# Order of single waits in a two-block transformer kernel: gates, last pair and first pair of the softmax attentions, their projection, banks of the second queries, last token tiles

## The reference

```python
def first_block(x, ...):
    z = rms_norm(x, norm1_g) @ w_in                      # glu | q | k | v | gate logits
    a = silu(rms_norm(causal_depthwise_conv(a_val * sigmoid(a_gate)), conv_norm_g))   # 31 taps
    y_a = a @ w_conv_out
    # three dilated window attentions over 16 heads of 64, mixed by the softmax of their log-sums
    o = einsum('gbsh,gbshd->bshd', softmax(stack(lses)), stack(outs))
    y_b = o @ w_attn_out
    g_a, g_b = split(sigmoid(gate_logits + gate_b))
    x = x + (g_a * y_a + g_b * y_b) @ w_out
    u_val, u_gate = split(causal_depthwise_conv(rms_norm(x) @ w_up))                  # 3 taps
    return x + (silu(u_gate) * u_val) @ w_down

def second_block(x, ...):
    # layer 0: softmax attention over the 128 keys that an index score picks; times silu(g); projection
    # layer 1: stick-breaking attention; times silu(g); projection
    # each followed by layer_norm(ALPHA * x + y)
```

## Time and profile before

| what | value |
|---|---|
| median of 3 runs | 1572.48 us (1572.32 to 1574.3) |
| profiled execution, its time | 1572.18 us |
| its span (first to last instruction) | 1570.4 us |
| PE busy | 1520.5 us, 97% of the span |
| DVE busy | 907.5 us, 58% |
| ACT busy | 520.4 us, 33% |
| POOL busy | 547.1 us, 35% |
| chain that ended last | PE 90%, DVE 5%, DMA 2%, ACT 2%, issue 1% |
| mean granted clock of PE | 0.994 of full speed |

### The profile page before, as it was taken

One profiled execution on the slowest core, in us unless ns is written; L12 is line 12 of the kernel. 1 busy time (PEld: TensorE's weight loads), 2 busy tenths in 40 slices (PEclk: granted clock), 3 DMA queues, 4 the chain that ended last, 5 costly groups with the idle time before them and its releaser, 6 DMA issues.

```text
span 1570.4 us, 19211 instructions
## 1 busy us (share of the span) xinstructions
PE 1520.5 (97%) x7506; PEld 1240.4 (79%) x7506; DVE 907.5 (58%) x1562; ACT 520.4 (33%) x1012; POOL 547.1 (35%) x662
## 2 busy tenths in 40 slices
PE   6999999999999999999999999999999989999996
PEld 5888888877777788888888887787777868888885
DVE  2899968478864243334310025896887451767765
ACT  4223234267741132222200012212776032444440
POOL 3222234421124444444444443344111334332221
PEclk9999999999999999999999999999999999999999
DMA  8999998854349788898988887788333768665655
GB/s 230 191 199 192 192 192 191 187 121 94 80 100 208 170 179 190 192 195 197 192 190 194 184 184 161 158 189 185 68 81 71 181 143 191 131 136 116 133 119 136
DMA packets 72969, 253.10 MB, mean 161 GB/s; under 512 B 7728, under 2 KB 11952, under 8 KB 72880
## 3 DMA queue, kind: packets, MB, share of 16 engines
q0 software_dynamic: 66528, 242.25, 71.4%
q1 hardware_dynamic: 5808, 7.53, 1.4%
q10 hardware_dynamic: 544, 2.10, 0.4%
HBM read 249.75 MB, written 2.10 MB: 160 GB/s over the span
## 4 chain that ended last, share of the span: by engine, by line
PE 90%; DVE 5%; DMA 2%; ACT 2%; issue 1%; POOL 0%; SPq 0%; DVEq 0%; ACTq 0%; POOLq 0%
PE PSUM L485 26%; PE PSUM L487 25%; PE PSUM L486 25%; PE PSUM L684 3%; PE PSUM L642 2%; PE PSUM L660 2%; PE PSUM L791 1%; PE PSUM L809 1%; PE PSUM L822 1%; PE PSUM L630 1%; DMA W_LO<-wstream 1%; DMA SMALLS<-small 1%; PE PSUM L956 1%; DVE QKV L1538 0%; PE PSUM L673 0%
## 5 line engine op out<-in xcount | busy, mean ns | idle before, releaser
L473 POOL DMA_DIRECT2D W_HI<-wstream x231 | 131.0, 567 | 860.9 <-PE PSUM L487 860.4
L485 PE MATMUL PSUM<-X_HI,W_HI 128*128 128x512 f32 x872 | 347.8, 399 | 4.0 <-DVE X_LO L1428 2.7
L487 PE MATMUL PSUM<-X_HI,W_LO 128*128 128x512 f32 x872 | 340.0, 390 | 0.0
L486 PE MATMUL PSUM<-X_LO,W_HI 128*128 128x512 f32 x872 | 339.9, 390 | 0.0
L465 POOL DMA_DIRECT2D W_LO<-wstream x231 | 206.9, 896 | 106.5 <-POOL W_LO L462 84.1
L462 POOL TENSOR_SCALAR W_LO<-W_HI 128x1024 fp32r<-128x1024 f32 x195 | 212.4, 1089 | 28.7 <-DMA W_HI<-wstream 25.5
L485 PE MATMUL PSUM<-W_HI,X_HI 128*128 128x512 f32 x544 | 212.8, 391 | 1.1 <-ACT QKV L1296 1.1
L486 PE MATMUL PSUM<-W_LO,X_HI 128*128 128x512 f32 x544 | 211.7, 389 | 0.0
L487 PE MATMUL PSUM<-W_HI,X_LO 128*128 128x512 f32 x544 | 211.7, 389 | 0.0
L485 PEld LDWEIGHTS PSUM<-X_HI,W_HI 128*128 128x128 f32 x872 | 163.3, 187 | 45.5 <-issue 9.2
L487 PEld LDWEIGHTS PSUM<-X_HI,W_LO 128*128 128x128 f32 x872 | 163.3, 187 | 35.2
(11 more groups left out here) (227 smaller groups left out, 2355.7 us busy)
## 6 DMA issues: line engine op xcount, KB each, us to landing
W_HI<-wstream POOLq DMA_DIRECT2D x231, 512.0 KB, 3.8
W_LO<-wstream POOLq DMA_DIRECT2D x231, 512.0 KB, 5.6
GATE_A<-x SPq DMA_DIRECT2D x4, 512.0 KB, 5.9
QKV<-x SPq DMA_DIRECT2D x8, 256.0 KB, 3.2
NORM_GAINS<-lnv ACTq DMA_DIRECT2D x2, 1024.0 KB, 6.5
out<-GATE_B SPq DMA_DIRECT2D x3, 512.0 KB, 2.6
CONST<-consts SPq DMA_DIRECT2D x1, 968.0 KB, 10.6
out<-GATE_B SPq DMA_DIRECT2D x2, 256.0 KB, 2.0
```

The costliest lines, as they stand in the source:

```text
L473: pool.dma_start(W_HI[:, n % SLOTS, :], wstream[n]).then_inc(w_hi_in[n % SLOTS], 16)
L485: pe.matmul(o, lh, rh, start=start, stop=False)
L486: pe.matmul(o, lh, rl, start=False, stop=False)
L487: return pe.matmul(o, ll, rh, start=False, stop=stop)
```

## The change

Six edits, all of order; no arithmetic, no instruction and no DMA is added or removed.

1. Gates of "a": DVE's `gates(i, 3)` moves from the end of pair i into pair i+1, behind its first `biased`, the reciprocal (`inverse`) and the two `pt_lo` of query block 2.
2. Last pair of "b": on ACT `pt_hi(7, 0)` and `pt_hi(7, 1)` come ahead of `low_products(6)`; on DVE `pt_lo(7, 0)`, `pt_lo(7, 1)` and `biased(7, 3)` come ahead of `both_parts(6)`.
3. First pair of both: PE's `turn_qk(1, 1)` moves behind `turn_p(0, 0)` and `turn_p(0, 1)`.
4. `attention_out`: each slab runs k = 0 to 7 in one go, slabs 0 and 1 too.
5. Second half of q2: one wait for each bank instead of one for all four.
6. out_b, second half: slab 2 runs for token tiles 0 and 1 before slab 3 is waited for.

(Edit 1 also stands behind the loop for pair 7, whose gate slab has no work for DVE.)

```diff
@@ t_half @@
-                pe.wait_ge(tile_free, free)
+                if not by_bank:
+                    pe.wait_ge(tile_free, free)
...
+                            if by_bank and k == 0:
+                                pe.wait_ge(tile_free, free - TT + 1 + t)
...
                 if tokens:
+                    if paired:
+                        slab_ready(s0 + kts // 2 - 2)
+                        products(kts // 2 - 2, 0)
+                        products(kts // 2 - 2, 1)
                     for t in range(TT):
                         for n in (kts // 2 - 2, kts // 2 - 1):
+                            if paired and t < 2 and n == kts // 2 - 2:
+                                continue
@@ softmax_attention, PE @@
-                    if i < PAIRS - 1:
+                    if 0 < i < PAIRS - 1:
                         turn_qk(i + 1, 1)
                     turn_p(i, 0)
                     turn_p(i, 1)
+                    if i == 0:
+
+                        turn_qk(1, 1)
@@ attention_out @@
-                for n in range(2):
-                    slab_ready(s0 + n)
-                    part(n, range(KT - 1))
-                for n in range(2):
-                    part(n, (KT - 1,)).then_inc(slab_done, 1)
-                pe.wait_ge(tile_free, t0)
-                for n in range(2, KT):
+                for n in range(KT):
+                    if n == 2:
+                        pe.wait_ge(tile_free, t0)
                     slab_ready(s0 + n)
                     part(n, range(KT)).then_inc(slab_done, 1)
@@ attention, ACT @@
-                    if i:
+                    if a == "b" and i == PAIRS - 1:
+                        pt_hi(i, 0)
+                        pt_hi(i, 1)
                         low_products(i - 1)
-                    pt_hi(i, 0)
-                    pt_hi(i, 1)
+                    else:
...
@@ attention, DVE @@
                         pt_lo(i - 1, 2, 0)
                         pt_lo(i - 1, 2, 1)
+                        if a == "a":
+                            gates(i - 1, 3)
...
-                    if i:
+                    if a == "b" and i == PAIRS - 1:
+
+                        pt_lo(i, 0)
+                        pt_lo(i, 1)
+                        biased(i, 3)
                         both_parts(i - 1)
-                    biased(i, 3)
-                    pt_lo(i, 0)
-                    pt_lo(i, 1)
+                    else:
...
-                    gates(i, 3)
+                    if a == "b":
+                        gates(i, 3)
```

More of the change, by code:

```diff
@@ L542, in f_phase, with t_half @@
                     turn(i, False)
-            def t_half(bank, s0, kts, hi, lo, free, ready=None, tokens=None, aside=None, slabs=None):
-                pe.wait_ge(tile_free, free)
+            def t_half(bank, s0, kts, hi, lo, free, ready=None, tokens=None, aside=None, slabs=None, by_bank=False, paired=False):
+                if not by_bank:
+                    pe.wait_ge(tile_free, free)
                 banks = bank if isinstance(bank, tuple) else range(bank, bank + TT)
@@ L868, in stick_attention @@
                 pe.wait_ge(sem("c_wt_lo"), 4 * PAIRS)
-                t_half(OUT_B_BANKS[1], s0 + KT // 2, KT, O_HI, O_LO, t0, tokens="out_b_token")
+                t_half(OUT_B_BANKS[1], s0 + KT // 2, KT, O_HI, O_LO, t0, tokens="out_b_token", paired=True)
             pe.wait_ge(const_in, 32)
@@ L965, in _ @@
             index_scores(0)
-            t_half(4, s0 + 4, KT, X_HI, X_LO, t0 + 4, scores_beside)
+            t_half(4, s0 + 4, KT, X_HI, X_LO, t0 + 4, scores_beside, by_bank=True)
             need(pe, "i_relu", 3 * IH)
@@ L1139, in attention @@
                         qk_hi(i + 1, 1)
-                    if i:
+                    if a == "b" and i == PAIRS - 1:
+                        pt_hi(i, 0)
+                        pt_hi(i, 1)
                         low_products(i - 1)
-                    pt_hi(i, 0)
-                    pt_hi(i, 1)
+                    else:
+                        if i:
+                            low_products(i - 1)
+                        pt_hi(i, 0)
+                        pt_hi(i, 1)
                     prob(i, 3, 0)
@@ L1572, in attention @@
                         qk_lo(i + 1, 1)
-                    if i:
+                    if a == "b" and i == PAIRS - 1:
+                        pt_lo(i, 0)
+                        pt_lo(i, 1)
+                        biased(i, 3)
                         both_parts(i - 1)
-                    biased(i, 3)
-                    pt_lo(i, 0)
-                    pt_lo(i, 1)
+                    else:
+                        if i:
+                            both_parts(i - 1)
+                        biased(i, 3)
+                        pt_lo(i, 0)
+                        pt_lo(i, 1)
                     if i:
```

## The result

| | kernel before | changed kernel |
|---|---|---|
| median, 5 runs each | 1573.69 us (1572.32 to 1574.3) | 1565.18 us (1562.48 to 1567.4) |
| ratio of the runs | | 0.9948, 95% interval 0.9938 to 0.9959 |
| profiled execution: time, span | 1572.18, 1570.4 us | 1566.73, 1564.9 us |

The changed kernel is 8.2 us faster by the ratio (6.4 to 9.8). I forecast 1566.3. A second series of five runs of it had a median of 1565.49, with a ratio of 0.996 (0.9947 to 0.9972). The profiled execution gained 5.5 us, and what follows is mostly about that gap and about the six terms.

A forecast was written before the change was run, and what follows sets the result against it. PE, busy 97% of the span, was taken as the bound. Terms 1.8 + 0.6 + 2.2 + 1.2 + 0.6 - 0.2 = 6.2 us gave 1566.0 profiled, 1566.3 as median; range 1563.9 to 1569.3.

The forecast's parts named there:

- DVE's chain hanging on PE: Attention a: DVE's chain starts with keys PE turned, so moving the gate gives 0.61 us per wait and leaves 1.38.
- the limit that I had named: First pair of a: scores(0, 3) needs biased(0, 2), so PE can start only at 319.12, gaining 0.3 us, not 1.0.
- DVE's sum: Last pair of b: DVE's steps added up let out_a start at 1205.15, 0.5 us earlier, after a new 2.1 to 2.2 wait.
- The wait lies midway between the two rows, so I take the middle: Last pair of b: clock kept gives 1.4 us, clock lost again gives -0.2; the middle, 0.6, was taken.
- my lower bound: Last pair of b: the least gain allowed for the new order, -0.2 us.
- PE starts slab 3 of tile 0 at 1549.0, 0.3 after 1548.71: Program end: 1.36 us of matmuls put ahead, 0.1 slow start saved, DVE starting 0.2 us later; the edit costs 0.2.
- at the end no wait for the last slab: Program end: a sign expected in the profile after, where before PE idled 0.91 us for that slab.
- rival (c): Last pair of b: PE keeps 2.4 GHz and another half-speed stretch goes; 0.8 + 1.2 us more, 1564.3; chance 0.12.
- (a): Attention pairs: waits of the gates and first-pair edits return, DVE's whole work setting the pace; gain 3.8, 1568.7 us; chance 0.14.
- (b): Attention output: another late thing appears, or the DMA doesn't come forward; gain 4.0, 1568.5 us; chance 0.09.
- (d): Attention a: DVE and POOL meet more often, seven at 1.35 us each; slower by 3.3, 1575.8 us; chance 0.02.

The follow-up runs named there:

- e3: The kernel before with only DVE's gates of query block 3 moved into the next pair in attention a: 1570.34 us, ratio 0.9986.
- e12: The kernel before with only the first-pair turns reordered and one wait per bank at the second queries: 1569.88 us, ratio 0.9984.
- e4: The changed kernel with the ACT and DVE order in the last pair of b put back as before: 1565.09 us, ratio 0.995.
- e2: The kernel before with only the attention output changed, each slab in one go: 1569.73 us, ratio 0.998.
- e1: The changed kernel with the new order at the end (out_b, second half) taken back: 1564.94 us, ratio 0.9948.
- e6: The changed kernel with a quarter of a gate slab moved from pair 6 to pair 7 of attention b: 1564.5 us, ratio 0.9947.
- e11: The changed kernel with HEAD_BIAS in two parts, gate-slab quarter moved to pair 7 of b, biased(6, 3) early and the new end order taken back: 1562.46 us, ratio 0.9936.
- e5: The changed kernel run and profiled once more, unaltered: 1565.49 us, ratio 0.996.
- e7: The changed kernel with DVE's output(i - 1) of attention a moved behind the first biased of the next pair: 1570.1 us, ratio 0.9987.
- e10: The changed kernel with a gate-slab quarter moved from pair 6 to 7 of b and DVE's biased(6, 3) ahead of both_parts(5): 1564.55 us, ratio 0.9948.

## Why the prediction was right, step by step

| edit | forecast | shown by the traces | from |
|---|---|---|---|
| 1 gates | 1.8 | 1.85 | A, e3 |
| 3 first pairs | 0.3 + 0.3 | 0.2 + 0.2 | A of e12; D of e4 (164.75) against before, e2, e3 (165.0, late slabs taken off) |
| 4 attention output | 2.2 | 2.5 (2.0 to 4.6) | B |
| 5 second queries | 1.2 | 1.16 | C |
| 2 last pair | 0.6 | -0.15 | D, e4 |
| 6 end | -0.2 | -1.0 | E, e1 |
| sum | 6.2 | 4.8 (4.3 to 6.9) | |

**Edits 1, 3 and 5** came out as worked out, edit 3 with 0.1 less in each pair. The waits left are 1.37, 1.40 and 1.41 in pairs 3, 6 and 7, and pair 4's is gone, as the account of DVE's chain hanging on PE asks. In the first pair of "a" the wait of 0.8 for QK_LO became one of 0.29 for `biased(0, 2)`, which is the limit that I had named.

**Edit 4.** The step was right: slab 0 finishes 21 matmuls earlier, the low part is there, and nothing new is late. The size was off for a reason that the one trace couldn't show. I took the length of the wait, 1.95, as a property of the order; it is one of the transfer. With the second DMA issued at the same distance from the beginning of the phase (468.45 in e12, 468.35 in before and e3) it was 1.69, 1.95 and 2.99 us, and the long one brought a half-speed stretch with it. Beside the 2.2 two more matmuls of before were slow, at the next slab, which makes most of the step to 2.5.

**Edit 2.** DVE's sum was right: `both_parts(6)` ran 1196.91 to 1198.31, PE waited 2.03 (I had 2.1 to 2.2), and 0.3 of the 0.5 at the start was won (from the first scores of "b" to `out_a` 114.15 us, in e4 114.42). Even this is mostly clock: in e12, with the old order and full speed, it is 114.20, so the 0.5 held the six slow turns of before's trace (1.17 us from their start to `out_a`, 0.81 in e12). The step that failed is "The wait lies midway between the two rows, so I take the middle". One of the two rows was a single draw: in the next pair of "a", behind a wait that cost no clock in before (2.00), the clock did fall in e2 (2.01). In the last pair it fell, as in ten of the eleven executions with a wait of 2.0 to 2.3 us there, and the stretch now lay wholly in the first slab of `out_a`: 24 matmuls took 7.15 us, 6.48 before, and 5.57 at full speed in e6. The result, -0.15, is my lower bound.

**Edit 6** is the term most wrong. The step "PE starts slab 3 of tile 0 at 1549.0, 0.3 after 1548.71" set the wait of 0.91 against the 1.36 put ahead of it. That wait was there in one execution of before's order; in e1, e2 and e12 there was none, in e3 0.38, in e11 0.29. Against before's own execution, with its late slab, the new order does lose the 0.2 that I had (E 52.41, and 52.60 in e5). Without a late slab the edit is all cost, and the cost is on DVE's path: its last stretch took 17.6 us after (1544.94 to 1562.54) as before, as I had said, and starts 1.0 later. One of my signs failed with this term: "at the end no wait for the last slab" holds in e5, but in the first profiled execution PE waited 0.22 us for it, and 0.27 for the one before.

**The sum against the medians.** By the traces the edits give 4.8 us at the usual transfer time, the medians 7.0 (1572.36 over the 55 later runs of before against 1565.33 over the ten of the changed kernel). Runs of before spread over 1568 to 1576. Part of the rest may be the clock, which would be rival (c) in another place: of the 55 runs of before 34 had a mean granted clock of 0.993 or less, of the changed kernel's ten 4. Among equal clocks the gain is 5.6 us at 0.993 (means 1572.9 of 28 and 1567.3 of 4) and 7.3 at 0.995 (1571.1 of 5 and 1563.8 of 5). Another part may be the long case of edit 4, which the changed kernel no longer has. How much each holds isn't settled: after the first norm's waits of 0.77 and 0.98 us, the same in all traces, a half-speed stretch followed in seven of fourteen, worth 1.7 us (C 542.8 against 541.1), with no rule that I can read from the rows. The forecast was 1.1 us from the first series and 0.8 from the second, although edits 2 and 6 were overrated by 1.6 together. That it came so near is in part luck: edit 4 gave 0.3 more, and what no term of mine held gave 2.2 by the medians. Nor is the distance in the time that of the gain: I had 6.2, the ratio says 8.2, and before's median was 1573.69 in that series, 1.2 above the 1572.48 that I started from.

**The rivals.** (a) and (b) did not happen. (d) did not either: four of eight L1553 were long, in the same four pairs as L1538 before, and the three moved gates took 0.67 to 0.68 each, so none of them met POOL. (c) did not come in the last pair, where the clock fell. But e7 shows that a meeting is real, and finds another instruction when one is moved.

## What to carry to other kernels

In these traces a wait for an engine of the same chain repeats from execution to execution within 0.1 us in the attentions (1.37 to 1.41, 2.03 to 2.04, 2.31) and within 0.2 at the second norm (2.52 to 2.68); a wait for a transfer is one draw of many (none to 0.91 us at the last slab in the old order). Take the first as a number and the second as a range, and look whether an edit pays when that wait is zero. Where an engine behind PE sets the end, as DVE does here, the matmuls put ahead of its first input are paid in time (six of them, 1.36 us of work, for 1.0 us). What the clock does behind a wait is a draw as well. A wait of 2.0 us ahead of dense work cost 1.4 to 1.6 us more by it, and 1.36 us of work placed in it was worth 1.9.

## What the hardware showed that I had not expected

- With a wait of 2.0 to 2.3 us ahead of `out_a` the clock fell to 1.2 GHz for a part of the first slab in ten of eleven traces and stayed in one; with 0.85 us it stayed in all three (e6, e10, e11). The fall costs 1.4 to 1.6 us. The length alone doesn't tell: in attention "a" it fell behind one of six waits of 2.0 us (before, e2, e12), and in e7 behind one of 1.23 that followed one of 0.71.
- The same DMA of a low part, issued at 468.35 in both kernels, made PE wait 1.95 us in one execution and 2.99 in another.
- The time goes with the mean granted clock of the whole run: before's runs average 1572.9 us at 0.993 (28 runs) and 1571.0 at 0.996 (9).
